# Retrieved rows scaled in place by ScalarE and summed by TensorE as fp32 transposes, in a two-layer decoder trunk with expert retrieval

## The reference

```python
def block(xb):                       # 128 tokens
    qh = (xb @ w_q).reshape(P_TOK_BLOCK, P_HEADS, 2, P_QDIM // 2)
    s = jnp.einsum('thpd,hpnd->thpn', qh, sub_keys).astype(jnp.float32)
    ...                              # per head: the 16 best of 128 x 128 experts, a gate for each
    u = u_tab[experts]
    v = v_tab[experts]
    act = jax.nn.gelu(jnp.einsum('td,thkd->thk', xb, u))
    return jnp.einsum('thk,thkd->td', gate * act, v)
```

## Time and profile before

| | |
|---|---|
| median of three runs | 3095.94 us |
| span of the profiled execution | 3088.5 us |
| around the span (median less span) | 7.4 us |
| TensorE matmul busy | 2705.7 us (88%) |
| VectorE busy | 2233.0 us (72%) |
| ScalarE busy | 1515.4 us (49%) |
| GpSimd busy | 1298.6 us (42%) |
| moved by DMA | 1194.54 MB, mean 387 GB/s |
| of it by the indirect fetches | 1073.81 MB |
| granted TensorE clock, mean | 0.96 of full |

### The profile page before, as it was taken

One profiled execution on the slowest core, in us unless ns is written; L12 is line 12 of the kernel. 1 busy time (PEld: TensorE's weight loads), 2 busy tenths in 40 slices (PEclk: granted clock), 3 DMA queues, 4 the chain that ended last, 5 costly groups with the idle time before them and its releaser, 6 DMA issues.

```text
span 3088.5 us, 30099 instructions
## 1 busy us (share of the span) xinstructions
PE 2705.7 (88%) x8304; PEld 1443.1 (47%) x8304; DVE 2233.0 (72%) x5560; ACT 1515.4 (49%) x4064; POOL 1298.6 (42%) x1254
## 2 busy tenths in 40 slices
PE   8969888998998989889998899899999878787777
PEld 6446553444564545554455455555455322222222
DVE  1337678997657888788766788888876767777664
ACT  2434344885434665565434565656444444444443
POOL 0014344554434444445444454454443444444442
PEclk9889999999999999999999999999999999999999
DMA  8029999999999999999999999999999999999997
GB/s 287 12 99 424 399 422 420 386 375 392 424 424 424 410 389 373 375 408 396 421 423 426 417 414 376 399 381 398 409 425 424 426 427 427 427 420 424 422 427 317
DMA packets 192647, 1194.54 MB, mean 387 GB/s; under 512 B 21344, under 2 KB 28512, under 8 KB 54752
## 3 DMA queue, kind: packets, MB, share of 16 engines
q0 software_dynamic: 147456, 1073.81, 84.5%
q1 hardware_dynamic: 45024, 118.82, 10.0%
HBM read 1189.38 MB, written 2.10 MB: 386 GB/s over the span
## 4 chain that ended last, share of the span: by engine, by line
PE 45%; DMA 24%; DVE 16%; ACT 9%; issue 4%; POOL 2%; POOLq 0%; DVEq 0%; SPq 0%; ACTq 0%
PE ps L1823 24%; DMA region_g<-in_uv_dram,experts 21%; DVE region_g L1313 7%; PE ps L1653 5%; PE ps L1685 2%; PE ps L1714 2%; PE ps L1682 2%; DMA region_a<-in_keys_dram 1%; PE ps L1732 1%; POOL region_g L674 1%; ACT x_res L947 1%; ACT L940 1%; DVE x_res L1322 1%; PE ps L1521 1%; ACT region_a L941 1%
## 5 line engine op out<-in xcount | busy, mean ns | idle before, releaser
L1823 PE MATMUL ps<-region_g,x_res 128*128 128x512 f32 x3648 | 1782.1, 619 | 271.7 <-ACT x_res L947 254.0
L674 POOL DMA_INDIRECT region_g<-in_uv_dram,experts x1024 | 1165.0, 1138 | 1571.9 <-PE ps L1823 1263.0
L1313 DVE CUSTOM_DVE_ANT_0 region_g<-region_g,region_h 128x1024 f32<-128x1024 f32 x1024 | 1258.5, 1231 | 493.1 <-DMA region_g<-in_uv_dram,experts 478.7
L1823 PEld LDWEIGHTS ps<-region_g,x_res 128*128 128x128 f32 x3648 | 672.6, 195 | 1093.9 <-issue 547.6
L940 ACT ACTIVATE region_a<-region_a 128x1 f32<-128x1 f32 x1024 | 206.4, 202 | 1231.6 <-DVE region_a L1313 1223.5
L947 ACT ACTIVATE x_res<-ident,region_a 128x128 f32<-128x128 f32 x912 | 366.2, 402 | 29.8
L941 ACT ACTIVATE region_a<-region_a,gate 128x1 f32<-128x1 f32 x1024 | 301.6, 295 | 33.3
L1653 PE MATMUL ps<-region_a 128*128 128x256 f32 x1024 | 244.9, 384 | 7.4 <-DMA region_a<-in_keys_dram 6.2
L1653 PEld LDWEIGHTS ps<-region_a 128*128 128x128 f32 x1024 | 197.0, 193 | 80.5 <-issue 51.5
L940 ACT ACT_TABLE_LOAD x128 | 164.2, 1283 | 13.7 <-DVE region_a L1313 11.5
L1322 DVE SCALAR_TENSOR_TENSOR x_res<-region_g,region_a,x_res 128x1024 f32<-128x1024 f32 x112 | 144.0, 1285 | 2.3 <-ACT region_a L941 2.3
(11 more groups left out here) (237 smaller groups left out, 2277.5 us busy)
## 6 DMA issues: line engine op xcount, KB each, us to landing
region_a<-in_w_q_dram SPq DMA_DIRECT2D x32, 1024.0 KB
region_a<-in_w_odd_dram SPq DMA_DIRECT2D x32, 1024.0 KB
region_g<-in_uv_dram,experts POOLq DMA_INDIRECT x1024
region_g<-in_w_even_dram SPq DMA_DIRECT2D x8, 1024.0 KB, 12.0
region_a<-in_w_even_dram SPq DMA_DIRECT2D x8, 1024.0 KB
region_a<-in_w_out_o_dram SPq DMA_DIRECT2D x8, 1024.0 KB
region_a<-in_keys_dram SPq DMA_DIRECT2D x32, 128.0 KB
region_g<-in_w_out_e_dram SPq DMA_DIRECT2D x4, 1024.0 KB, 4.9
```

Source lines behind the costliest of these rows:

```text
L674: g.indirect_dma_start(out=gath[:, s % NBUF, :], out_offset=None, in_=uv[s // (2 * PHASE)], in_offset=bass.IndirectOffsetOnAxis(ap=experts ...
L1313: v.tensor_tensor_reduce(out=u_, in0=u_, in1=XNr[n // P_HEADS % 3], scale=1.0, scalar=0.0, op0=ALU.mult, op1=ALU.add, accum_out=dots[:, c: ...
L1823: i = t.matmul(PS[:, j, :], diag[:, pe_n(s) % NBUF, :], gath[:, s % NBUF, D_MODEL + j * 512:D_MODEL + (j + 1) * 512], start=first, stop=last)
```

## The change

The weights no longer go into a diagonal. ScalarE multiplies the v half of the buffer by the weight in place (128x1024 in, 128x1024 out; before, 128x128), and no longer waits for a free diagonal buffer. TensorE turns each of the eight 128x128 chunks of the scaled row and lets PSUM add the turned chunks over the slots, so banks 0 and 1 hold the sum with channels on partitions. At a block's end VectorE copies the sum out of PSUM into `sumT` (the plane that held the diagonals), TensorE turns it back with eight transposes, and VectorE adds it to X as before, one slot later than before. The 112 slots on VectorE stay as they are.

```diff
-        diag = X[:, TB, :].rearrange("p (a b) -> p a b", a=NBUF)
+        sumT = X[:, TB, :]
...
                     link(i)
-                    after(act, slot_done, pe_n(s) - NBUF)
-                    a.activation(diag[:, pe_n(s) % NBUF, :], ident, ACT.Copy, scale=wts[:, c:c + 1]
-                                 ).then_inc(diag_ready.sem, 1)
+                    v_ = gath[:, s % NBUF, D_MODEL:ROW]
+                    a.activation(v_, v_, ACT.Copy, scale=wts[:, c:c + 1]).then_inc(scaled_row.sem, 1)
...
+            def sums_out(b):
+
+                after(dve, slot_done, pe_n(BLOCK * (b + 1) - 1))
+                v.tensor_copy(v3(sumT, 2), PS[:, 0:2, :]).then_inc(sumT_out.sem, 1)
+
             def block_out(b):
 
-                after(dve, slot_done, pe_n(BLOCK * (b + 1) - 1))
+                dve.wait_ge(sum_back.sem, sum_back.at(b))
                 after(dve, vd_done, dve_n(BLOCK * (b + 1) - 1))
...
                 if s % BLOCK == 1 and s > BLOCK:
+                    sums_out(s // BLOCK - 1)
+                if s % BLOCK == 2 and s > BLOCK:
                     block_out(s // BLOCK - 1)
...
             threads.run(SLOTS)
+            sums_out(2 * TB - 1)
             block_out(2 * TB - 1)
...
-                if first:
-                    if b:
-                        after(pe, acc_out, b - 1)
-                pe.wait_ge(diag_ready.sem, diag_ready.at(pe_n(s)))
-                for j in range(2):
-                    i = t.matmul(PS[:, j, :], diag[:, pe_n(s) % NBUF, :],
-                                 gath[:, s % NBUF, D_MODEL + j * 512:D_MODEL + (j + 1) * 512], start=first, stop=last)
+                if first and b:
+                    sums_turned(b - 1)
+                    after(pe, acc_out, b - 1)
+                pe.wait_ge(scaled_row.sem, scaled_row.at(pe_n(s)))
+                for c in range(KC):
+                    i = t.matmul(PS[:, c // 4, c % 4 * P:(c % 4 + 1) * P],
+                                 gath[:, s % NBUF, D_MODEL + c * P:D_MODEL + (c + 1) * P], ident,
+                                 start=first and c % 4 == 0, stop=last, is_transpose=True, skip_group_check=True)
                 i.then_inc(slot_done.sem, 1)
+
+            def sums_turned(b):
+
+                pe.wait_ge(sumT_out.sem, sumT_out.at(b))
+                for c in range(KC):
+                    i = t.transpose(PS[:, c // 4, c % 4 * P:(c % 4 + 1) * P], sumT[:, c * P:(c + 1) * P], ident)
+                i.then_inc(sum_back.sem, 1)
```

More of the change, by code:

```diff
@@ L267, in build @@
         routed, gexp_in, gexp_out = event("routed"), event("gexp_in"), event("gexp_out")
-        dots_ready, w_ready, diag_ready = event("dots_ready"), event("w_ready"), event("diag_ready")
+        dots_ready, w_ready, scaled_row = event("dots_ready"), event("w_ready"), event("scaled_row")
         slot_done, vd_done = event("slot_done"), event("vd_done")
         acc_out, f_ss, fin_done = event("acc_out"), event("f_ss"), event("fin_done")
+        sumT_out, sum_back = event("sumT_out"), event("sum_back")
         gathered = [sem(f"gathered{i}") for i in range(NBUF)]
@@ L1275, in gates_of @@
                 if n >= 2:
-                    after(dve, diag_ready, pe_n(TOPK * (n - 1) - 1))
+                    after(dve, scaled_row, pe_n(TOPK * (n - 1) - 1))
                 link.need(m)
@@ L1834, in _ @@
             threads.run(SLOTS)
+            sums_turned(2 * TB - 1)
 def kernel(**inputs):
```

## The result

The changed kernel takes 3138.49 us (median of 4 runs, 3135.73 to 3141.09) against 3095.55 us of the kernel before in the same comparison (3090.88 to 3097.05). The ratio is 1.0141, 95% interval [1.0127, 1.0156]: 43 us slower, with the sign as forecast, but 33 us above the forecast of 3105 and 13 us above the range. The profiled execution took 3136.11 us with a span of 3134.1 us, 45.6 us more than before; the granted clock was 0.811 in the mean, 0.96 before. Two executions among all the runs lie far outside the rest and enter no ratio: one of e4 (4123.86 us) and one of the kernel before beside it (14210.67 us).

A forecast was written before the change was run, and what follows sets the result against it. The DMA rings were taken as the bound from 212 us on. Attention stage +14, recurrence -10, block ends +2 and end +3 summed to +9 us, forecast 3105 us; the range for 8 in 10 was 3083 to 3125.

The forecast's parts named there:

- the sign as forecast: Whole kernel: the change makes it slower, chance 0.52, against 0.28 for the same and 0.20 for faster.
- the DMA share: By stage: 1.01 means full rings; read as reached in four of six stretches, where a faster TensorE wins nothing.
- The recurrence: Both recurrence stages: of 23 us lost, 10 come back as TensorE's queue shrinks; bounds -23 to +5.
- Scaling +0.75, product -0.86: Recurrence, per row in us: ScalarE longer, TensorE shorter, so the path from dot product to free buffer stays as long.
- Clear in the mean, with a lag of a few rows behind each burst: First recurrence stage: ScalarE goes from 254.6 to 353 of 450 us busy and still has room.
- the upper bound: Recurrence stages: +5 us, if ScalarE's bursts now hold back VectorE's waits.
- The attention stage: ScalarE gets 171.3 us of work in 160, 19 us late; net +14 us after credit, bounds 0 to +31.
- The 5 us of credit: Attention stage: a shorter TensorE product shortens the wait behind mixer work, taken off ScalarE's 19 us lag.
- The first stretch: From 212 us, before the attention stage: DMA share 1.01 taken as full, so no loss was counted.
- Block ends: Seven times an extra VectorE copy and turning back, about 3.5 us each, mostly hidden by buffers: +2 us, bounds 0 to +8.
- The end: After the last row: longer scaling, copy and turning back all lie on the path: +3 us, bounds +2 to +5.
- The clock: Rival, recurrence: transposes lower TensorE's clock; 10 to 20 us (3120 us) if brief, over 3300 us if lasting; chance 0.07.

The follow-up runs named there:

- e4: Changed kernel with GpSimd's row fetches of slots 40 to 51 held until the dot product three slots before: 3131.51 us, ratio 1.0117.
- e2: Changed kernel with ScalarE weighing only 128 of each row's 1024 columns, the others added unweighed: 3085.66 us, ratio 0.9974.
- e8: Kernel before with rows weighed in place, only 128 of 1024 columns, added by the old matmuls with the identity: 3093.72 us, ratio 1.0002.
- e1: Kernel before with ScalarE scaling the full row in place, added by the old matmuls with the identity, no transposes: 3159.66 us, ratio 1.0215.
- e7: Changed kernel with ScalarE weighing only 128 of 1024 columns in slots 256 to 767 (the recurrence): 3103.11 us, ratio 1.0026.
- e3: Changed kernel with ScalarE weighing only 128 of 1024 columns in slots 88 to 191 (attention part and what follows): 3120.65 us, ratio 1.0089.

## Why the prediction was wrong

**Direction and mechanism.** Right in sign: ScalarE's longer instruction outweighs TensorE's shorter one. The scaling took 1149 ns (1148 forecast). One reading of the earlier trace rows was wrong, without effect on the sum: the DMA share is 1.01 in three of the six stretches, not four.

**The recurrence, the step that failed.** I forecast -10 us with bounds of -23 and +5; it was +7. "Scaling +0.75, product -0.86, so the path from dot to free buffer is as long as before" was right about rows and left out what else is in ScalarE's queue. "Clear in the mean, with a lag of a few rows behind each burst" took an average load (353 of 450 us forecast, 359 measured) for a cover. The runs show two large terms in place of a small one. By the lengths of the stage, the transposes win 20 us beside a short instruction (e2 against e8) and 28 us beside a long one (after against e1), and ScalarE's length costs 32 us (after against e2), 36 us (after against e7) and 40 us (e1 against e8), mostly through VectorE's waits. I had named these waits only as the upper bound. Before, at the earlier trace rows, ScalarE was at 57% and seemed to have room; VectorE at 83% had none to give.

**The attention stage, undersized.** +14 forecast (0 to +31), +26 measured (+30 and +31 in e7 and e4). ScalarE's part was sized well: 19 us late was the forecast, and by the lengths of the stage its longer instruction costs 16 to 22 us here (after against e3, e7 against e2), 20 beside the old matmuls (e1 against e8). It reaches VectorE by the same kind of wait, here for the exponentials of the attention. VectorE's waits from the dot product of slot 88 to that of slot 184, before and after:

```profile
DVE coef L1077 <- ACT region_a L793: 1.1, 1, 1.1
...
DVE coef L1077 <- ACT region_a L794: 12.1, 8, 3.0
```

The 5 us of credit for a shorter TensorE wait had the wrong sign: the transposes cost 7 us here with a short instruction (e2 against e8) and 6 with a long one (after against e1). In e2 ScalarE waits 17.1 us for TensorE's attention work in these slots, against 9.8 before, and TensorE's matmuls of 256 columns there (L1620, L1612 before) take 453 ns against 400, with the clock at 0.84 against 0.97. So the lower clock may be the cause of these 6 to 7 us. That is not shown: no run has the transposes at the old clock, and 6 to 7 us is little more than the spread of single executions.

**The first stretch, not foreseen.** From 212 to 560 us I counted on a full DMA share to hide everything. A share of 1.01 says that the rings carry all they can, not that the transfer that an engine needs next comes first. That missed 9 us at slot 88.

**Block ends.** +2 forecast (0 to +8). In the last stage, with a full DMA share, their cost is nothing (41.8 us late at slot 768, 41.6 at 1023); those in the earlier stages were not measured apart.

**The end.** +3 forecast (+2 to +5), +4.0 measured: 17.7 us from the last dot product to the end of the span, against 13.7. The timeline of the changed kernel from the last row on:

```profile
3118.17 1.15 ACT L948 ACTIVATE region_g<-region_g,region_a 128x1024 f32<-128x1024 f32 x1
3119.37 1.57 PEld L1831 LDWEIGHTS ps<-ident,region_g 128*128 128x128 f32 x8 [0.86 <-ACT region_g L948]
3119.37 1.97 PE L1831 MATMUL ps<-ident,region_g 128*128 128x128 f32 x8 [0.46 <-ACT region_g L948]
3121.38 1.22 DVE L1328 COPY x_res<-ps 128x1024 f32<-128x1024 f32 x1 [3.81 <-PE ps L1831]
3122.66 1.57 PEld L1840 LDWEIGHTS ps<-ident,x_res 128*128 128x128 f32 x8 [1.72 <-DVE x_res L1328]
3122.66 1.97 PE L1840 MATMUL ps<-ident,x_res 128*128 128x128 f32 x8 [1.32 <-DVE x_res L1328]
3124.67 1.22 DVE L1335 TENSOR_TENSOR x_res<-x_res,ps 128x1024 f32<-128x1024 f32 x1 [2.06 <-PE ps L1840]
```

Against the earlier trace rows the scaling is 0.75 longer, the copy 1.22 and the turning back 1.97 are new, and both turnings run at the lower level, so that the row's own, 1.97 us, wins nothing over the 1.98 of before.

**The sum, as measured:** +9 + 26 + 7 + 0 + 4 = 46, against +45.6 of span.

**The clock.** Busy TensorE time was 2278.8 us and not 1950, for two reasons: a row cost 1226.0/912 = 1.34 us in the mean and not 1.09, 228 us in all, and the rest of TensorE's work took 1052.8 us, the turning back of the sums included, against 923.6 before. In the recurrence the clock fell to 0.85 from 0.97. I had put 10 to 20 us on that if it was brief, and over 3300 us on the whole if it lasted. Nothing of the kind came: e2 wins 20 to 25 us in the recurrence at the same clock (0.86), and TensorE, at 73% in these stages of the changed kernel, has idle time. What the transposes would win there at the upper level no run shows.

## What to carry to other kernels

Before lengthening an instruction on an engine that is "clear in the mean", list what stands in that engine's queue behind it and which busier engine waits for that; here 0.75 us per row on ScalarE at 57% cost 32 to 40 us in the recurrence, mostly through a VectorE at 83%, more than the transposes won. Trading time between two engines inside a chain that has the same length afterwards is not neutral: each engine's other duties pay or gain too. And a full DMA share says nothing of a late slab that shares the rings with several large gathers.

## What the runs showed of the hardware

**Accumulating fp32 transposes** of 128x128 take the same as plain ones: eight in 1.97 us at the lower level (end of the timeline above) and in 1.09 us at the upper one (TensorE's timeline of the changed kernel at 348 us), where the earlier trace rows has 1.97 and 1.09 for the plain kind.

**The clock.** With rows of eight transposes and little else on TensorE the granted clock is 0.67 in the mean (2540 to 2640 us), between the two levels of 1.2 and 2.4 GHz (0.5 and 1.0); before, with matmuls of 512 columns and TensorE 78% busy, it was 1.00. The Trainium skill, "TensorE: Matmul & The Clock Gate", Part 4, says that the full clock does not engage for transpose-mode work. This trace agrees in direction, but not fully: 0.67 is not the lower level's 0.5, so for a third of that time the upper level was granted, and the start of the program had a dense run of transposes alone followed by the upper level.

**A slab beside gathers.** The same 1120-KB load, issued within a few us of the same time, was complete 26 us after its issue in the kernel before and 39 us after it in the changed one, each time with row fetches of 1 MB on the way: in the mean of the first 12 us 0.9 of them in the one and 2.0 in the other.
